# Output projections of a three-block kernel in three rounded passes instead of one fp32 pass

## The reference, cut to what matters

```python
def gla_mixer(...):     # block 0
    o = rmsnorm(o, norm_g) * jax.nn.silu(g).reshape(B, S, GLA_HEADS, GLA_DV)
    return o.reshape(B, S, GLA_VD) @ w_out
def lru_mixer(...):     # block 1
    y = hs.astype(h.dtype) * jax.nn.gelu(gate_br)
    return y @ w_out
def gated_merge(...):   # second_block
    return (g_m * (y_m @ w_m) + g_a * (y_a @ w_a) + g_s * (y_s @ w_s)) @ w_o
# around them:
    sh1, sc1, g1, sh2, sc2, g2 = jnp.split(cond @ ada_w[i] + ada_b[i], 6, axis=-1)
    x = x + g1[:, None] * mix
    h = modulate(rmsnorm(x, norm_ffn_g[i]), sh2, sc2)
```

## Time and profile before

| | us |
|---|---|
| median of 3 runs (lowest, highest) | 1894.09 (1893.87, 1896.95) |
| profiled execution, its own time | 1892.52 |
| its span, first to last instruction | 1890.6 |
| PE busy, weight loads busy | 1787.2, 1408.2 |
| DVE busy, ACT busy | 1089.6, 759.8 |
| projection matmuls (L680) busy | 83.6 |
| mean granted TensorE clock, share of full speed | 0.974 |

### The profile page before, as it was taken

The page is one execution under the profiler, slowest core; times in us unless marked ns, Lnnn a source line. Parts: engine busy times, 40 slices in busy tenths (PEclk is TensorE's granted clock), DMA queues, the critical chain, the costliest instruction groups (busy, mean ns, idle before and its releaser), DMA issues.

```text
span 1890.6 us, 23412 instructions
## 1 busy us (share of the span) xinstructions
PE 1787.2 (95%) x9437; PEld 1408.2 (74%) x9437; DVE 1089.6 (58%) x1593; ACT 759.8 (40%) x976; POOL 0.2 (0%) x4
## 2 busy tenths in 40 slices
PE   6999999999998989999999979999999998989998
PEld 4786777777876847777777766987645776879998
DVE  2332554447886354644468868438855563449886
ACT  3212433244664233323356665336633432034443
POOL 0000000000000000000000000000000000000000
PEclk9999899999999999999999999999989999989999
DMA  9847577668884685777778862235621322445550
GB/s 360 274 152 261 213 265 284 268 267 309 309 316 156 224 303 196 287 292 287 279 261 303 313 213 67 90 112 196 208 81 51 112 82 74 133 156 179 180 177 23
DMA packets 178596, 392.95 MB, mean 208 GB/s; under 512 B 11318, under 2 KB 102057, under 8 KB 162105
## 3 DMA queue, kind: packets, MB, share of 16 engines
q1 hardware_dynamic: 176814, 389.58, 57.8%
q10 hardware_dynamic: 1674, 1.88, 0.3%
HBM read 390.39 MB, written 1.05 MB: 207 GB/s over the span
## 4 chain that ended last, share of the span: by engine, by line
PE 87%; DVE 6%; ACT 4%; DMA 2%; issue 1%; SPq 0%; DVEq 0%; ACTq 0%
PE bank L849 18%; PE bank L539 12%; PE bank L877 9%; PE bank L1284 7%; PE bank L680 4%; PE bank L1086 4%; PE bank L1295 3%; PE bank L861 3%; PE bank L566 3%; PE bank L640 3%; PE bank L583 2%; DMA ring<-in_ada_w_dram 2%; PE bank L1240 2%; PE bank L892 2%; PE bank L549 1%; PE bank L597 1%
## 5 line engine op out<-in xcount | busy, mean ns | idle before, releaser
L2086 DVE TENSOR_TENSOR parts<-ring,parts 128x2048 fp32r<-128x2048 f32 x144 | 329.1, 2291 | 166.8 <-ACT parts L1527 165.7
L849 PE MATMUL bank<-parts 128*128 128x512 f32 x1536 | 369.3, 400 | 9.6 <-DVE parts L2162 4.0
L1527 ACT ACTIVATE parts<-ring 128x2048 fp32r<-128x2048 f32 x144 | 275.2, 1917 | 230.5 <-PE bank L849 164.2
L849 PEld LDWEIGHTS bank<-parts 128*128 128x128 f32 x1536 | 292.7, 193 | 79.4 <-issue 18.6
L1377 ACT ACTIVATE work<-bank 128x256 f32<-128x256 f32 (+3 forms) x223 | 97.9, 446 | 452.8 <-PE bank L539 135.8
L539 PE MATMUL bank<-hh,ring 128*128 128x256 f32 x896 | 200.7, 384 | 3.7 <-ACT hh L1420 3.7
L539 PEld LDWEIGHTS bank<-hh,ring 128*128 128x128 f32 x896 | 171.2, 192 | 32.0 <-issue 8.6
L877 PE MATMUL bank<-parts 128*128 128x512 f32 x768 | 179.4, 391 | 3.7 <-DVE parts L2111 3.7
L877 PEld LDWEIGHTS bank<-parts 128*128 128x128 f32 x768 | 143.4, 188 | 36.7 <-DVE parts L2111 4.1
L1284 PE MATMUL bank<-parts 128*128 128x256 f32 x1056 | 131.0, 286 | 7.6 <-DVE parts L2626 7.6
L1284 PEld LDWEIGHTS bank<-parts 128*128 128x128 f32 x1056 | 130.0, 196 | 8.4 <-DVE parts L2626 8.4
(11 more groups left out here) (293 smaller groups left out, 2191.4 us busy)
## 6 DMA issues: line engine op xcount, KB each, us to landing
ring<-in_moe_w_gate_dram SPq DMA_DIRECT2D x64, 1024.0 KB, 6.5
ring<-in_moe_w_up_dram SPq DMA_DIRECT2D x64, 1024.0 KB, 7.3
ring<-in_moe_w_down_dram SPq DMA_DIRECT2D x64, 1024.0 KB, 5.9
ring<-in_ada_w_dram SPq DMA_DIRECT2D x48, 1024.0 KB, 7.2
ring<-in_w_in_dram SPq DMA_DIRECT2D x32, 1024.0 KB, 5.9
ring<-in_w_mod_dram SPq DMA_DIRECT2D x24, 1024.0 KB, 7.4
ring<-in_w_up_dram SPq DMA_DIRECT2D x22, 1024.0 KB, 5.1
ring<-in_gla_w_in_dram SPq DMA_DIRECT2D x12, 1024.0 KB, 7.9
```

Of the source, the lines that this page charges most:

```text
L849: ins = pe.matmul(bank[:, :], xg[:, a_, k, tile * P:(tile + 1) * P], w[b_][:, j, :], start=k == 0 and n == 0, stop=k == KT - 1 and n == 2)
L1527: act.activation(moe_w[:, n % 3, 0, :], ring[:, g % RING, :], ACT.Identity)\
L2086: dve.tensor_tensor(moe_w[:, n % 3, 1, :], ring[:, (MOE_AT[layer] + AT[key]) % RING, :], moe_w[:, n % 3, 0, :].bitcast(F32), sub).then_inc ...
```

## The change

All three projections run in the three rounded passes. Sources (`g_o`, `l_h`, `g_acc`) are split tile by tile as they arise: ACT `y_high` (L1483 of the changed kernel), DVE `y_low` (L1988). Weights are split by half slots: ACT `out_highs` (L1477), DVE `out_lows` (L1981), which writes the low part over the slot in the ring. High parts of weights have two buffers. PE waits per half slot for `out_low` and, in the first tile, per source tile for `y_low`.

The first two `gla_out` and `lru_out` slots now come earlier in the slot order, between the last modulation chunks. PE still runs all modulation chunks first; `next_slot` lets it take slots out of the ring's order.

```diff
-        for chunk in BEFORE_GLA_OUT:
+        for i, chunk in enumerate(BEFORE_GLA_OUT):
             yield from mod(*chunk)
-        for j in range(4):
+            if i in (1, 2):
+                yield "gla_out", wide(A["gla_w_out"][0], 256 * (i - 1))
+        for j in range(2, 4):
             yield "gla_out", wide(A["gla_w_out"][0], 256 * j)
...
-        for chunk in BEFORE_LRU_OUT:
+        for i, chunk in enumerate(BEFORE_LRU_OUT):
             yield from mod(*chunk)
-        for j in range(4):
+            if i in (3, 4):
+                yield "lru_out", wide(A["lru_w_out"][0], 256 * (i - 3))
+        for j in range(2, 4):
             yield "lru_out", wide(A["lru_w_out"][0], 256 * j)
...
-            def residual_out(what, rhs, which, j):
-
-                w = weights(what, KT)
+            def residual_out(what, which, j):
+
+                n = OUT.index(next_slot(what))
                 for m in range(2):
+                    pe.wait_ge(sem("out_low"), 2 * n + m + 1)
+                    w = out_high_half(n, m), out_half(n, m, of=ring_low)
                     ps = to_dve.fill(pe)
                     for k in range(KT):
-                        ins = pe.matmul(ps[:, 0:T], w[:, k, m * P:(m + 1) * P], rhs(k), start=k == 0, stop=k == KT - 1)
+                        if j == 0 and m == 0:
+                            pe.wait_ge(sem("y_low"), y_count(which, k))
+                        for i, (a_, b_) in enumerate(PASSES):
+                            ins = pe.matmul(ps[:, 0:T], w[a_][:, k, :], out_parts[which][1 + b_][:, k, :],
+                                            start=k == 0 and i == 0, stop=k == KT - 1 and i == 2)
                     close(to_dve, ins)
...
+            def out_highs(n):
+
+                g = OUT[n]
+                act.wait_ge(landed[g % RING], 16 * (g // RING + 1))
+                for b in range(2):
+                    if n % 4 >= 2:
+                        act.wait_ge(*out_used[n - 2, b])
+                    act.activation(out_high_half(n, b), out_half(n, b), ACT.Identity).then_inc(sem("out_high"), 1)
...
             for j in range(4):
                 take_mod()
-            squares(lambda k: sq[:, k, 0:T], residual_in(0))
+                y_high(0, 2 * j, g_o)
+                y_high(0, 2 * j + 1, g_o)
+                if j > 1:
+                    out_highs(j - 2)
+            out_squares(0, lambda k: sq[:, k, 0:T])
...
-            for chunk in BEFORE_GLA_OUT:
+            for i, chunk in enumerate(BEFORE_GLA_OUT):
                 take_mod(*chunk)
-            residual(mods[:, 0, 16:24])
+                if i == 0:
+                    y_low(0, 6, g_o)
+                    y_low(0, 7, g_o)
+                if i > 1:
+                    out_lows(i - 2)
+            residual(0, mods[:, 0, 16:24])
...
                             tt(dst, dst, g_tmp, add)
-                            ts(dst, dst, 0.5, None, mul, done=sem("merged"))
-            residual(mods[:, 2, 16:24])
+                            ts(dst, dst, 0.5, None, mul, done=sem("y_raw"))
+                            if j:
+                                y_low(2, 4 * half + j - 1, g_acc)
+                y_low(2, 4 * half + 3, g_acc)
+                if half == 0:
+                    out_lows(8)
+                    out_lows(9)
+            residual(2, mods[:, 2, 16:24])
```

More of the change, by code:

```diff
@@ L243, in build @@
     SLOTS = list(plan())
+    OUT = [g for g, (what, _) in enumerate(SLOTS) if what in ("gla_out", "lru_out", "w_out")]
+    out_used = {}
     MOE_AT = [next(i for i, (what, arg) in enumerate(SLOTS) if what == "moe" and arg[0] == layer) for layer in range(2)]
@@ L430, in build @@
         g_th = room(24, T)
+        out_parts = []
+        for at in (19728, 16408, 8192):
+            again(at)
+            out_parts.append((room(2, 2, D, of=work_rounded), room(KT, T, of=work_rounded),
+                              room(KT, T, of=work_rounded) if at != 19728 else None))
+            assert used[0] <= ROOM - 1024 - ROW_TILES * P
+        again(G_V_AT)
+        out_parts[0] = (*out_parts[0][:2], room(KT, T, of=work_rounded))
         again(FF_PARTS)
@@ L513, in _, with next_slot @@
             to_act, to_dve = act_banks(), dve_banks()
-            slot = [0]
+            left, slots = list(range(len(SLOTS))), []
+            def next_slot(what):
+                g = next(i for i in left if SLOTS[i][0] == what)
+                left.remove(g)
+                slots.append(g)
+                return g
             def weights(what, kt):
-                g = slot[0]
-                assert SLOTS[g][0] == what, (g, SLOTS[g][0], what)
+                g = next_slot(what)
                 pe.wait_ge(landed[g % RING], 16 * (g // RING + 1))
-                slot[0] += 1
                 return ring[:, g % RING, :].rearrange("p (k n) -> p k n", k=kt)
             def free_slot(sem_, value, back=1):
-                freed[slot[0] - back] = (sem_, value)
+                freed[slots[-back]] = (sem_, value)
             def close(banks_, ins):
@@ L1081, in half_linear @@
                 if m == 0:
-                    held[:] = weights("u", KT), slot[0] - 1
+                    held[:] = weights("u", KT), slots[-1]
                 w, g = held
@@ L1319, in _ @@
                 marks["out", t] = to_act.n
-            assert slot[0] == len(SLOTS)
+            assert not left
         @block.sync
@@ L1631, in _ @@
                 take_mod()
-            squares(lambda k: sq[:, k, 0:T], residual_in(1))
+                y_high(1, 2 * j, l_h)
+                if j > 1:
+                    out_highs(4 + j - 2)
+            out_squares(1, lambda k: sq[:, k, 0:T])
             experts(1)
@@ L1775, in _ @@
             inverses(2, 256)
-            squares(lambda k: f_sq[:, k, 0:T], residual_in(2))
+            for k in range(4):
+                y_high(2, k, g_acc)
+            out_highs(8)
+            out_highs(9)
+            for k in range(4, 8):
+                y_high(2, k, g_acc)
+            out_squares(2, lambda k: f_sq[:, k, 0:T])
             inverse(D)
@@ L1910, in residual @@
                                                   in1=x[:, k, :], op0=mul, op1=add))
+                    if k in (1, 3):
+                        out_lows(4 * stage + k // 2 + 2)
             norm(gains[:, 0, :])
@@ L2254, in _ @@
             dve.wait_ge(sem("lru_gelu"), 1)
-            stt(l_g, l_r, 1.0, l_g, add, mul)
-            stt(l_h, l_h, 0.5, l_g, mul, mul, done=sem("lru_y"))
-            for chunk in BEFORE_LRU_OUT:
+            for chunk in BEFORE_LRU_OUT[:2]:
                 take_mod(*chunk)
-            residual(mods[:, 1, 16:24])
+            for k in range(0, KT, 2):
+                at = slice(k, k + 2)
+                stt(l_g[:, at], l_r[:, at], 1.0, l_g[:, at], add, mul)
+                stt(l_h[:, at], l_h[:, at], 0.5, l_g[:, at], mul, mul, done=sem("y_raw"))
+                if k:
+                    y_low(1, k - 2, l_h)
+            y_low(1, 6, l_h)
+            for i, chunk in enumerate(BEFORE_LRU_OUT[2:]):
+                take_mod(*chunk)
+                if i > 1:
+                    out_lows(4 + i - 2)
+            residual(1, mods[:, 1, 16:24])
             gain(3, 1, 32, col("norm_ffn_g", 8, 8))
```

69 lines of the change are left out of this document (47 added, 22 removed).

## The result

| | median, us | lowest to highest, us | runs |
|---|---|---|---|
| before | 1893.87 | 1892.83 to 1896.95 | 5 |
| after | 1903.94 | 1901.05 to 1907.19 | 5 |

The ratio is 1.0050 (95% interval 1.0036 to 1.0065): slower, by 10 us, as forecast (1903.5). The profiled execution of the new kernel took 1901.60 us, with a span of 1899.8 us at a mean granted clock of 0.966; before it was 1892.52, 1890.6 and 0.974. Two executions of later rounds in a slower state of the chip (3018.67 us of the kernel with fillers, 3503.52 us of the kernel before) are left out of all ratios. In the new kernel L640 has become L673 (modulation chunk), L652 L685 (its transposes), L680 L718 (projection), L597 L630 (norm sum), L539 L574, L1377 L1412 (ACT's copy) and L1831 L2702.

A forecast was written before the change was run, and what follows sets the result against it. PE was taken to bound the kernel (87% of the chain), with loads setting the first two projections' starts. Terms +6.9, +7.5 and -5.0 sum to +9.4 us: 1901.9 for the profiled execution, 1903.5 for the median; range 1896.5 to 1910.

The forecast's parts named there:

- The sum: Whole kernel: first projection +6.9, second +7.5, third -5.0 us, together +9.4 us; chance 0.47.
- The pace of the rounded matmul, 119 ns: All projections: 192 rounded matmuls at 119 ns take 22.9 us instead of 27.9, saving 5.0 us three times.
- a quarter of an fp32 matmul: Rival, all projections: each rounded matmul takes 109 ns, 6.0 us less in all, +3.4 us, 1897.5; chance 0.04.
- The first start: First projection: PE starts at 178.7, 7.9 us later, the last modulation slot landing 5.6 us later.
- The queue of splits: ACT and DVE work after the last modulation slot delays PE's start: 2.3 us in the first projection, 2.6 in the second.
- The second start: Second projection: PE starts 8.5 us later than 700.36, its last modulation slot landing 5.9 us later.
- The stall at the third slot: First and second projection: PE waits 2.0 us for the third slot, loaded only after slot one is free.
- The clock: Starts of first and second projection: granted clock falls to 1.2 GHz while PE idles, costing 2.0 us each.
- The rival with a second drop in the stall: First two projections: third slot 1.9 us later, second clock drop 1.4 us, each; +16.0 us, 1910; chance 0.12.
- The third projection: Third projection: bank wait and saved source wait nearly cancel, leaving -5.0 us; bounds -6.4 and -3.0.
- The bank wait: Third projection's branches: DVE's four low halves hold up its work on PE's tiles, stalling PE 1.0 us.
- The rival of the load stream: First two projections: moved slots fit in the stream, the saving arrives three times, -15.0 us, 1879; chance 0.07.

The follow-up runs named there:

- fillers: The changed kernel plus matmuls of constants, results unused, where PE would idle ahead of late chunks and the first tile; 1900.64 us, ratio 1.0037 to before.
- third only: Against the kernel before: only the third projection in three passes, first two in fp32 with slots in the old order; 1887.92 us, ratio 0.9962.
- order only: The changed kernel's slot order alone, all three projections in one fp32 pass from the raw source, no splits; 1907.45 us, ratio 1.0068 to before.
- One early: The changed kernel with one output slot instead of two ahead of the last modulation chunk, first and second projection; 1893.25 us, ratio 0.9993 to before.
- splits ahead: The changed kernel with last source tiles' high parts ahead of ACT's last copy, first low halves ahead of DVE's last reduces; 1898.02 us, ratio 1.0016 to before.
- Mixed: Three passes, but old slot order and the first of four slots in one fp32 pass in the first two projections; 1881.59 us, ratio 0.9933 to before.

## Why the prediction was right

**The sum.** Forecast +9.4 us on the profiled execution, measured +9.1 (1901.60 - 1892.52). By the anchors of the new kernel's own trace the three stretches give +7.7, +6.6 and -2.6, together +11.7, and the rest of the kernel, which was not changed, took 2.6 us less than in the trace of before. So the closeness of 9.1 to 9.4 is in part luck: differences between two executions cancelled. What the change itself does is better read with the third projection's -5.4 of "third only": +8.9, where 6.9, 7.5 and -5.0 stood. The mechanism stands in each term, the size of the terms within one and a half microseconds.

**The pace of the rounded matmul, 119 ns: right.** Windows of the new kernel, L718 alone (PE, PEld, clock, DMA share, GB/s), third projection first:

```profile
1661.00:1684.40 23.40, 22.96 (x192) 22.86 (x192) 1.00 0.55 181
180.00:207.00 27.00, 23.95 (x188) 23.75 (x189) 0.94 0.69 241
716.00:743.00 27.00, 24.40 (x192) 24.20 (x192) 0.94 0.69 245
```

22.96 us for 192 are 119.6 ns, and all three windows add up to 71.3 us, near the 68.6 forecast at full clock: the two that hold a stretch at the lower clock have 2.4 us more. The Trainium skill (FP8 and Floating Point Precision, TensorE Precision Notes) says that true FP32 makes four passes through the array. From that I had an estimate of a quarter of an fp32 matmul for each rounded one, 109 ns; this trace does not agree, its rounded matmul takes 119.6. PEld is as busy as PE, 22.86 us: each short matmul has a weight load beside it. Whether that sets the pace was not tried.

**The first start: right, by its parts.** Forecast 7.9 us later, without the clock; measured 8.7. The last modulation slot came 5.9 us later after the anchor (15.9 against 10.0), 5.7 on the mean of four traces, 5.6 forecast. The queue of splits added 2.3 (5.83 from there to the start, 3.55 in order only), 2.3 forecast. The other 0.5 is the clock: the last half chunk took 0.87 longer (1.93 for 1.06), and part of that went into gaps that were there before.

**The second start: 7.7 for 8.5 with the clock on top.** The loads came sooner after their anchor than counted: the last slot's wait ended 27.8 us after it, against 23.3 before (697.30 - 673.96), 4.4 later where I had 5.9. The queue added 2.7, forecast 2.6. Order only has 6.8 at the start. From one trace to the next the landing varies here by 1.1 us with the old order and by 1.8 with the new one; "before" has the latest of the first four and "after" the earliest of the second four. On the means the two moved slots cost 6.0, so the term was right and this pair of traces reads it low. (One early came 1.4 us sooner there, not 2.9, for the same reason in part.) The 708.9 of the prediction leaves out that the first projection's delay moves the second; in the trace it starts at 716.49.

**The stall at the third slot: right.** Forecast 2.0 us; measured 2.28 and 2.11. From SP's issue to ACT's start on it passed 5.5 us, 5.3 forecast, and then the two half splits as counted. One early, where it is gone, shows that it depends on the second moved slot: nothing can be asked for until slot one's tiles are through.

**The clock: right in kind, forecast 2.0 for each.** First projection: 0.9 in the chunk and about 1.6 in the first tile (start to end 26.8 us, less 22.96 of matmuls and 2.28 of stall); the second has the same 0.9 and 1.6. Holding the clock gave back 2.5 and 2.3 from the landing to the end, 2.7 and 1.0 from the anchor. By run times it is 2.5 of the 4.0 us, with an interval too wide for more. The rival with a second drop in the stall did not come about in this trace (1.00 at 194 to 196); with the splits ahead it did, with a first tile at full clock in exchange.

**The third projection: right.** -5.4 us by third only, and the same within 0.2 in the five other kernels below it in the table. The bank wait I priced at 1.0 is the 0.88 at 1647.74. The new kernel's own trace has only -2.6: it took 2.9 us longer than those six, 2.7 of them ahead of the mixer's first input projection, at the lower clock and in code that was not changed.

**The rival of the load stream.** It asked for both starts to shift by less than 7.0 us together. Order only shifts them by 12.9. Mixed shifts them by nothing and has the gain.

## What to carry to other kernels

In this kernel a cheaper form of a matmul that needs its operands prepared kept its whole saving only behind the point where the operands had arrived. Ahead of it, each slot moved forward in the ordered stream delayed the last modulation slot by its full time (about 3 us), and the slots left where they were exposed the preparation of the first (3.3 us). The way out was neither order: run the first piece in the costly form that needs no preparation, and prepare the rest beside it. It is worth a try wherever a projection follows a wait for DMA, even where DMA is 2% of the chain; other kernels were not tried here.

## What the runs showed of the hardware

Waits of 2.28 and 2.11 us for the third slot left the clock whole in the change (1.00 at 194 to 196), while waits of 2.65 and 2.31 us at the same places in the kernel with the splits ahead brought the lower level, the first for about 6 us (0.50 at 192 to 198). 2.28 us held and 2.31 us fell: a gap of this size has no fixed price. Nor does the fall always lie in the gap: the change's first tile began at full clock behind 2.41 us of idle time and was slowed half a microsecond later. Matmuls whose results nobody needs held the clock up when they filled the waits for loads (last half chunk 1.06 instead of 1.93 us), even with 1.5 us left between them and the work. The single most costly thing was neither: two loads of 1 MB, 5.7 us, in a stretch where the page's shares show DMA as almost free.
